# A hybrid decoder step on one core: key projections before branch linears, softmax sums and an output copy moved on VectorE, output halves taken in turn

## What is computed

```python
for l in range(DEPTH):                       # DEPTH = 2
    f = mixer_front(xp, pos_p, p)            # h = rmsnorm(x); z = h @ w_in, split into q, ckv, kr, u, v, gq, gk, gv, ...
    h_a = mla_prompt_attn(...)               # 8 heads: k = ckv @ w_uk, softmax(q k^T) v, causal, 512 x 512
    h_b, _ = gmlp_mix(f['u'], f['v'], p)     # u * (w_s v + b), 8 groups of 64 channels, chunks of 128 tokens
    o_c, s_c = gla_chunked(...)              # gated linear attention, 4 heads of 64 x 128
    xp = merge_and_ffn(xp, h_a, h_b, h_c, f['gate'], p)
    ...                                      # the same for the 8 sample tokens:
    h_a = mla_sample_attn(...)               # softmax over 32 pages of 128 cached tokens per sequence,
                                             # o_lat = probabilities @ cached latents
    o_c, s_c = gla_recurrent(...)
```

## Time and profile before

| what | value |
|---|---|
| median of 3 runs | 2017.96 us (2010.59 to 2018.74) |
| profiled execution | 2016.56 us, span 2014.9 us, mean granted clock 0.989 |
| TensorE busy | 1986.1 us (99%) |
| DVE, ACT, POOL busy | 1010.6, 712.8, 273.9 us |
| TensorE's waits for another engine or a DMA, the three largest | 4.9, 4.4 and 1.8 us in total |
| layer 1, stages 1 to 4 | about 15 to 500 us; layer 2 about 1012 to 1497 us |

### The profile page before, as it was taken

The page is one execution under the profiler, slowest core; times in us unless marked ns, Lnnn a source line. Parts: engine busy times, 40 slices in busy tenths (PEclk is TensorE's granted clock), DMA queues, the critical chain, the costliest instruction groups (busy, mean ns, idle before and its releaser), DMA issues.

```text
span 2014.9 us, 48295 instructions
## 1 busy us (share of the span) xinstructions
PE 1986.1 (99%) x20222; PEld 1898.0 (94%) x20222; DVE 1010.6 (50%) x1575; ACT 712.8 (35%) x1141; POOL 273.9 (14%) x520
## 2 busy tenths in 40 slices
PE   9999999999999999999999999999999999999998
PEld 9989988889999999999999899887999999999998
DVE  7765422376656444433367653324675554444333
ACT  5464122365333222222235631413642332222221
POOL 0004555400000000000000055563000000000000
PEclk9999999989999999999999999999999999999999
DMA  6428999932433333323353399998224332333232
GB/s 226 162 75 272 339 344 360 332 98 67 129 103 95 88 93 93 95 87 90 97 183 129 110 298 344 326 369 293 81 62 136 105 95 85 94 95 95 87 94 73
DMA packets 140976, 322.34 MB, mean 160 GB/s; under 512 B 24420, under 2 KB 72087, under 8 KB 140247
## 3 DMA queue, kind: packets, MB, share of 16 engines
q10 hardware_dynamic: 46944, 147.87, 23.9%
q1 hardware_dynamic: 69238, 100.05, 14.5%
q0 software_dynamic: 24576, 71.34, 10.1%
HBM read 307.08 MB, written 12.08 MB: 158 GB/s over the span
## 4 chain that ended last, share of the span: by engine, by line
PE 93%; DVE 2%; DMA 2%; ACT 1%; SPq 1%; issue 1%; ACTq 0%; DVEq 0%
PE PS L1957 27%; PE PS L1959 26%; PE PS L1958 26%; PE PS L2234 3%; PE PS L2262 3%; PE PS L2010 2%; DMA kp<-in_cache_keys 1%; SPq L2623 1%; PE PS L2125 0%; PE PS L2289 0%; PE PS L2390 0%; PE PS L2428 0%; PE PS L1996 0%; DMA xT<-in_x_t 0%; PE PS L2017 0%
## 5 line engine op out<-in xcount | busy, mean ns | idle before, releaser
L1957 PE MATMUL PS<-hh,wh 128*128 128x260 f32 x3008 | 864.7, 287 | 2.2 <-issue 1.0
L1959 PE MATMUL PS<-hl,wh 128*128 128x260 f32 x3008 | 855.2, 284 | 0.0
L1958 PE MATMUL PS<-hh,wl 128*128 128x260 f32 x3008 | 854.6, 284 | 0.0
L1957 PEld LDWEIGHTS PS<-hh,wh 128*128 128x128 f32 x3008 | 572.2, 190 | 16.8 <-issue 14.4
L1959 PEld LDWEIGHTS PS<-hl,wh 128*128 128x128 f32 x3008 | 572.4, 190 | 0.0
L1958 PEld LDWEIGHTS PS<-hh,wl 128*128 128x128 f32 x3008 | 571.7, 190 | 0.3
L725 DVE TENSOR_TENSOR wl<-raw,wh 128x1024 fp32r<-128x1024 f32 (+4 forms) x326 | 351.3, 1079 | 306.0 <-ACT wh L1481 305.2
L1481 ACT ACTIVATE wh<-raw 128x1024 fp32r<-128x1024 f32 (+4 forms) x326 | 304.7, 937 | 528.8 <-PE PS L1959 521.3
L1957 PE MATMUL PS<-fh,wh 128*128 128x260 f32 x704 | 199.5, 283 | 0.0
L1959 PE MATMUL PS<-fl,wh 128*128 128x260 f32 x704 | 198.9, 282 | 0.0
L1958 PE MATMUL PS<-fh,wl 128*128 128x260 f32 x704 | 198.8, 282 | 0.0
(11 more groups left out here) (363 smaller groups left out, 2808.6 us busy)
## 6 DMA issues: line engine op xcount, KB each, us to landing
raw<-in_wpack ACTq DMA_DIRECT2D x238, 512.0 KB, 3.6
kp<-in_cache_keys POOLq DMA_DIRECT2D x256, 144.0 KB, 4.4
kp<-in_cache_keys SPq DMA_DIRECT2D x256, 144.0 KB, 4.6
vpg<-in_cache_vals SPq DMA_DIRECT2D x256, 128.0 KB, 4.8
vpg<-in_cache_vals POOLq DMA_DIRECT2D x256, 128.0 KB, 4.9
raw<-in_wpack ACTq DMA_DIRECT2D x48, 256.0 KB, 3.4
raw<-in_wpack ACTq DMA_DIRECT2D x16, 384.0 KB, 3.2
x_keep<-xT SPq DMA_DIRECT2D x2, 2080.0 KB, 9.7
```

Of the source, the lines that this page charges most:

```text
L1957: pe.matmul(out, w[0], x[0], start=first, stop=False)
L1958: pe.matmul(out, w[1], x[0], start=False, stop=False)
L1959: return pe.matmul(out, w[0], x[1], start=False, stop=last)
```

## The change

Four edits, none of which alters what is computed.

1. At h = 0 and h = 2 of the prompt stage the key projection (k1, k2) goes in front of the linear (v3, u1) instead of behind it, on TensorE and in the order of the weight slabs; the calls of `weights` on DVE and ACT follow.
2. DVE makes the page softmax sums and their reciprocal at c = 4 of the page loop instead of behind it.
3. At c = 7 DVE copies `O` to `Oacc` between `difference(5)` and `decayed(3)`, instead of behind `difference(6)` and the sums.
4. In `mix_tokens` and in U the loop over the two output halves (partitions 0 to 63 and 64 to 127) becomes the inner one.

```diff
@@ -264,10 +264,10 @@
         if h == 6:
             groups.extend(["pt6b", "ql"])
             continue
+        if h == 0 or h == 2:
+            key((h + 2) // 2)
         if h in PROMPT_FILLERS:
             lin(PROMPT_FILLERS[h])
-        if h == 0 or h == 2:
-            key((h + 2) // 2)
         if h == 4:
             lin("q7")
         if h == 7:
@@ -983,9 +983,9 @@
                 branch_row(2)
                 for h in range(4):
                     if h == 0:
-                        weights(si["v3"])
+                        weights(si["uk1"])
                     maxima(h + 1)
-                    weights(si[PROMPT_FILLERS[h]])
+                    weights(si[f"uk{(h + 2) // 2}" if h % 2 == 0 else PROMPT_FILLERS[h]])
                     if h == 1:
                         branch_sum(2)
                         branch_sum(3)
@@ -996,7 +996,7 @@
                     normalise(h + 1)
                     if h % 2 == 0:
                         keys((h + 2) // 2)
-                        weights(si[f"uk{(h + 2) // 2}"])
+                        weights(si[PROMPT_FILLERS[h]])
                         query_row(h + 3)
                     else:
                         query_row(h + 3)
@@ -1194,6 +1194,10 @@
                         dve.wait_ge(*upto("pe pt3n"))
                         for i in range(3):
                             difference(i)
+                    if c == 4:
+                        dve.wait_ge(*upto("exps 3"))
+                        over_blocks(lc[:, :, :], ALU.add)
+                        dve.reciprocal(rec[:, :], by_row[:, 0:2]).then_inc(*mark("dve_step", "rec"))
                     if c == 6:
                         for i in range(2):
                             decayed(i)
@@ -1201,20 +1205,17 @@
                     merged(1, c)
                     if c == 7:
                         dve.wait_ge(*upto("read V47"))
-                        for i in (2, 3):
-                            decayed(i)
-                            difference(i + 3)
+                        decayed(2)
+                        difference(5)
+                        dve.wait_ge(*upto("pe O"))
+                        dve.wait_ge(*upto("rec"))
+                        for g in range(2):
+                            ins = dve.tensor_scalar(Oacc[:, g, :], bank("O")[:, 256 * g:256 * g + 256], rec[:, g:g + 1], None, ALU.mult)
+                        ins.then_inc(*mark("dve_evac", "free O"))
+                        decayed(3)
+                        difference(6)
                     if c < 7:
                         weights(si[VALUE_GATES[c]])
-                dve.wait_ge(*upto("exps 3"))
-                over_blocks(lc[:, :, :], ALU.add)
-                dve.reciprocal(rec[:, :], by_row[:, 0:2]).then_inc(*mark("dve_step"))
-                dve.wait_ge(*own())
-                dve.wait_ge(*upto("pe O"))
-                for g in range(2):
-                    ins = dve.tensor_scalar(Oacc[:, g, :], bank("O")[:, 256 * g:256 * g + 256], rec[:, g:g + 1], None, ALU.mult)
-                ins.then_inc(*mark("dve_evac", "free O"))
-
                 def spread_queries():
                     dve.wait_ge(*upto("pe O"))
                     dve.memset(gqb[:, :, :, :], 0.0).then_inc(*mark("dve_step"))
@@ -2283,9 +2284,9 @@
                     pe.wait_ge(*upto("free vt23"))
                     for i in range(4):
                         begin(f"mx{i}")
-                        for e in range(2):
-                            r = slice(64 * e, 64 * e + 64)
-                            for c in range(4):
+                        for c in range(4):
+                            for e in range(2):
+                                r = slice(64 * e, 64 * e + 64)
                                 ins = pe.matmul(bank(f"mx{i}")[r, 128 * c:128 * c + 128],
                                                 vtok[:, c, 128 * i + 64 * e:128 * i + 64 * e + 64], wsT[:, 2 * i + e, :],
                                                 start=True, stop=True)
```

## The result

The changed kernel takes 2022.32 us (median of 11 runs, 2019.23 to 2029.44); the kernel before took 2014.19 us beside it (11 runs, 2009.78 to 2020.55). (The prediction counted from the profiled execution of before, 2016.56 us, which lies 2.4 us above the median measured beside the changed kernel.) The profiled execution took 2024.79 us, its span is 2023.1 us.

The account below looks back on a forecast made before the run. The prediction took TensorE, busy 1986.1 of 2014.9 us, to bound the kernel. Its terms, +9.0 - 2.2 - 1.2 + 0 + 1.7 = +7.3 on 2016.56, gave 2023.9 us, range 2013.5 to 2031.5.

Parts of the forecast that it names:

- Part 1: Key projections moved ahead of linears: bank stalls of 3.5 and 2.2 us, +11.4, minus 2.4 from earlier scores: +9.0 us.
- The delay of 0.55 us: At h = 2, the larger conversion before DVE's maxima delays the exponentials 0.55 us; stall 2.2 us, 1.6 without it.
- rival (b): At k1 and k2, the bank wait does not bind: 2009 to 2011 us; chance 0.08.
- Part 2: Softmax sums and `Oacc` copy earlier: D0's 2.19 us wait goes, `Vt` copies then hold g01; 1.1 us a layer, -2.2.
- Part 3: Output halves alternate: U gains 0.6 us a layer, -1.2; mixing's 0.8 us booked at 0, lost to key-page waits.
- rival (c): Stalls taken back at the key-page wait, which swallows 4.9 us of the delay: 2019.0 us; chance 0.1.
- Part 4: Granted clock: two new falls behind the 3.5 us stalls, +3.4, one fewer at D, -1.7; together +1.7 us.
- Rival (a): Idle time behind k1, k2 lowers the clock: all four stalls followed by falls, nothing back at D: 2029.0 us; chance 0.2.

Follow-up runs that it names:

- e6: Changed kernel with k1's group in PSUM bank 5 instead of bank 2, k2 as in the changed kernel: 2011.76 us, ratio .9976 to the kernel before.
- e5: Changed kernel with key projections back behind the linears and ACT's `Vt` copies ahead of its last exponential: 2010.66 us, ratio .9971 to the kernel before.
- e8: Kernel before with every token-mixing matmul issued twice: 2023.95 us, ratio 1.0041 to the kernel before.
- e3: Kernel before with only the output halves alternating in mixing and U: 2013.06 us, ratio .9981 to the kernel before.
- e1: Kernel before with only the key projections k1 and k2 moved ahead of the linears v3 and u1: 2032.31 us, ratio 1.0075 to the kernel before.
- e4: Changed kernel with the key projections put back behind the linears, all else kept: 2006.61 us, ratio .9952 to the kernel before.
- e10: Kernel before with the eight transposes of Vt1 issued three times, in the place of D0's idle time: 2009.96 us, ratio .9967 to the kernel before.

## Why the prediction came out right, and where it did not

**Part 1, the stalls: right.** Forecast 3.5 and 2.2 us, 11.4 in all; measured 3.34 and 1.87, 10.5 in all. The bank's last reader was the right thing to read, and e6 shows it by taking it away. The delay of 0.55 us booked for the wider conversion at h = 2 did not arrive: 1.87 is nearer to the bound without it, 1.6. The wait for `kxl` went; rival (b) is out.

**Part 2, the next releaser: wrong.** The step put `Vt` in the place of `Oacc` and took 1.1 us a layer as the gain. Counted from the end of the `Vt` transposes, g01 starts 0.7 us (layer 1) and 0.9 us (layer 2) earlier. ACT's copy does end 0.24 us before Ot in layer 1 of the changed kernel, but e5 takes it away and Ot stays where it was. In layer 2 the copies did hold Ot (1.16 us) and g01 (0.26 us), but without them, in e5, the stop behind g01's first six matmuls is 2.61 us where it was 0.81. The binding resource was the instruction block, which the kernel before already waited for unseen: the wait for `Oacc` covered most of it, and 0.26 and 0.83 us of `issue` were what stood out. The Trainium skill (Runtime: NRT & Kernel Launch, section "Instruction fetch mechanics") states blocks of 16 KiB, 256 instructions, and that crossing from one to the next is mostly hidden; the size agrees with the 160 packets here, and behind 256 instructions in 1.3 us the crossing was not hidden.

**Part 3, mixing booked at 0: wrong.** The sizes were right (3.65 for 3.7, 1.90 for 1.9), but the step that let the key-page wait swallow mixing's gain is refuted by e8, and by e3 at equal clock: the loads shift with TensorE's work. The same runs refute rival (c). The part brought 2.8 us where 1.2 were booked.

**Part 4, the clock: wrong in place and size.** The sum allowed one stretch less at D and two more behind the stalls, +1.7 us. In the runs, part 2 takes away 12 us at half clock, and part 1 adds 14 (e1) to 19 (after against e4). The step looked only at the stretch next to D and not at the ones through the decay levels up to 451 us, which went as well in the profiled execution of the changed kernel (27.3 us at half clock from D to U before, none after). Rival (a), three or more falls behind the stalls, is what the profile shows at k1 and k2, but its other condition, that nothing comes back at D, failed.

**The sum.** Forecast +7.3, measured +8.1, and the agreement is in part luck. Part 1 was forecast at 9.0 + 3.4 = 12.4 and cost 16 to 17; parts 2 and 3 were forecast at -2.2 - 1.2 - 1.7 = -5.1 and brought -9.2. Both were too small by 4 us, with opposite signs. The mechanism of part 1, the one that decides the sign, was right by its own evidence (e6).

## What to carry to other kernels

Before a group is moved ahead of the work that used to stand in front of it, look up who last reads its PSUM bank: here one bank number was worth 12 us, and the reorder paid nothing beyond noise even with the right bank. On a kernel whose TensorE is busy 98 to 99% of the span, price an idle gap at its length plus the work lost at 1.2 GHz behind it, and read the granted clock of the whole following stage, not only of the next microseconds. Where a burst of small matmuls is followed by idle time, look for a packet of the instruction queue that landed just before the end of it. When an engine resumes for `issue`, or a named releaser ended just before it, take the suspected releaser away before believing in it.

## What the runs showed of the hardware

- Useless matmuls in an idle gap made the kernel faster: e10 is 5.3 us below before with 4 us more TensorE work.
- The spread of one kernel's runs goes mostly with the granted clock, 1.6 us for each 0.001 of its mean (106 runs of before). The medians of e4 and e5, two kernels with the same work, lie 4 us apart, with intervals that overlap, and nothing of it is left at equal clock (2014.1 both).
- Small matmuls can outrun the instruction supply: 256 instructions in 1.3 us were followed by up to 3.27 us of idle time, which ended about 1.3 us after the next 16 KB packet landed. TensorE's instructions come in such packets, one for each 253 of its matmuls and weight loads in all 14 traces, and the one that is needed begins only when the 256 instructions ahead of it are begun (layer 1: 1.0 to 1.5 us later in twelve kernels).
- Alternating the output halves of 64 rows takes 64 records from 4.47 to 3.65 us and 32 from 2.50 to 1.90 us with a contraction over 128 rows, where 32 records with a contraction over 8 take 1.89.
